# Two transformer blocks in split fp32r precision: three 256-wide matmuls per k-tile in place of a 512-wide and a 256-wide one

## What is computed

```
# block 1                                          # block 2
z = rms_norm(x) @ w_in          # 2048 x 11264      proj = rms_norm(x) @ w_in_2       # 2048 x 9216
y_a = hgrn2_scan(...) * silu(hg)  # 8 heads         y_a = gmlp(u, v)                  # 8 groups
y_b = chunk_band_attention(...)   # 16 heads        y_b = neighbourhood_attn(...)     # 16 heads
merged = gate_a * (y_a @ w_branch_a) + gate_b * (y_b @ w_branch_b)
h = x + merged @ w_out                              (the same in block 2)
h = h + relu(rms_norm(h) @ w_up)**2 @ w_down        x = x + (silu(gate) * val) @ w_down_2
                                                    # gate, val: 3-tap convolution of rms_norm(x) @ w_up_2
```

## Time and profile before

| | us |
|---|---|
| median of 3 runs | 3141.75 |
| lowest and highest | 3140.42, 3149.58 |
| the profiled execution's span | 3139.2 |
| its first matmul starts after | 9.2 |

### The profile page before, as it was taken

The page is one execution under the profiler, slowest core; times in us unless marked ns, Lnnn a source line. Parts: engine busy times, 40 slices in busy tenths (PEclk is TensorE's granted clock), DMA queues, the critical chain, the costliest instruction groups (busy, mean ns, idle before and its releaser), DMA issues.

```text
span 3139.2 us, 53753 instructions
## 1 busy us (share of the span) xinstructions
PE 2927.3 (93%) x16379; PEld 2496.7 (80%) x16379; DVE 2169.0 (69%) x3324; ACT 1515.2 (48%) x2293; POOL 1680.3 (54%) x1105
## 2 busy tenths in 40 slices
PE   5999999989999999999988999899899999999997
PEld 4777777778788888888876777777787788888886
DVE  5777777777568655556577666656747888878885
ACT  5544555556444444444463444445555444444454
POOL 4444445445655666656673445444374455555554
PEclk9999999999999999999999999999999999999998
DMA  5455555545556666666754555565565566666664
GB/s 160 144 146 145 145 145 146 146 140 165 172 173 177 191 190 186 185 183 192 202 148 135 151 155 162 144 163 154 155 188 156 166 182 183 189 177 190 187 182 123
DMA packets 1016035, 519.81 MB, mean 166 GB/s; under 512 B 28980, under 2 KB 1014700, under 8 KB 1015596
## 3 DMA queue, kind: packets, MB, share of 16 engines
q1 hardware_dynamic: 1014032, 513.90, 57.5%
q10 hardware_dynamic: 1820, 3.65, 0.3%
HBM read 515.35 MB, written 2.13 MB: 165 GB/s over the span
## 4 chain that ended last, share of the span: by engine, by line
PE 54%; DVE 27%; issue 9%; ACT 7%; DVEq 1%; DMA 0%; ACTq 0%; SPq 0%; POOL 0%; POOLq 0%
PE acc L401 24%; PE acc L403 12%; DVE w_lo L1157 6%; PE psX L401 5%; PE psT L401 5%; ACT w_hi L737 4%; PE psX L403 2%; PE psT L403 2%; DVE work L1163 2%; DVE work L1534 2%; DVE hT L1362 1%; DVE hT L1361 1%; DVE work L1521 1%; DVE work L1520 1%; DVE HS L1280 1%
## 5 line engine op out<-in xcount | busy, mean ns | idle before, releaser
L1049 POOL TENSOR_TENSOR w_lo<-w_raw,w_hi 128x512 fp32r<-128x512 f32 (+1 forms) x960 | 1548.2, 1625 | 1385.5 <-ACT w_hi L737 1381.5
L1157 DVE TENSOR_TENSOR w_lo<-w_raw,w_hi 128x512 fp32r<-128x512 f32 (+1 forms) x960 | 906.6, 950 | 688.6 <-ACT w_hi L737 634.6
L737 ACT ACTIVATE w_hi<-w_raw 128x1024 fp32r<-128x1024 f32 (+1 forms) x960 | 995.4, 1050 | 601.1 <-PE acc L403 467.4
L401 PE MATMUL acc<-XU,w_hi 128*128 128x512 f32 x3488 | 1256.7, 402 | 26.6 <-DVE work L1163 18.7
L403 PE MATMUL acc<-XU,w_lo 128*128 128x256 f32 x3488 | 983.6, 282 | 0.0
L401 PEld LDWEIGHTS acc<-XU,w_hi 128*128 128x128 f32 x3488 | 662.0, 190 | 195.7 <-DVE w_lo L1157 18.5
L401 PE MATMUL acc<-XY,w_hi 128*128 128x512 f32 x2112 | 768.6, 405 | 44.6 <-DVE work L1163 18.4
L403 PEld LDWEIGHTS acc<-XU,w_lo 128*128 128x128 f32 x3488 | 665.5, 191 | 1.1
L403 PE MATMUL acc<-XY,w_lo 128*128 128x256 f32 x2112 | 598.9, 284 | 0.0
L401 PEld LDWEIGHTS acc<-XY,w_hi 128*128 128x128 f32 x2112 | 404.0, 191 | 151.1 <-DVE w_lo L1157 23.6
L403 PEld LDWEIGHTS acc<-XY,w_lo 128*128 128x128 f32 x2112 | 407.2, 193 | 0.1
(11 more groups left out here) (250 smaller groups left out, 2993.5 us busy)
## 6 DMA issues: line engine op xcount, KB each, us to landing
w_raw<-in_w_in SPq DMA_DIRECT2D x320, 512.0 KB, 3.9
w_raw<-in_w_up SPq DMA_DIRECT2D x300, 512.0 KB, 4.4
w_raw<-in_w_down SPq DMA_DIRECT2D x208, 512.0 KB, 4.3
w_raw<-in_w_out SPq DMA_DIRECT2D x64, 512.0 KB, 3.9
w_raw<-in_w_branch SPq DMA_DIRECT2D x32, 512.0 KB, 3.8
w_raw<-in_w_branch_a SPq DMA_DIRECT2D x16, 512.0 KB, 3.8
w_raw<-in_w_branch_b SPq DMA_DIRECT2D x16, 512.0 KB, 3.8
bias<-in_rel_bias SPq DMA_DIRECT2D x8, 384.0 KB, 5.1
```

The source lines that it names most:

```text
L401: nc.tensor.matmul(bank[:, :], hi[:, k, col:col + P], X[:, k0 + k, :], start=first and k == 0, stop=False, skip_group_check=True)
L737: act.activation(w_hi[s][:, 0:n], w_raw[s][:, 0:n], ACT.Copy).then_inc(hi_done, 1)
L1049: nc.gpsimd.tensor_tensor(w_lo[s][:, n // 2:n], w_raw[s][:, n // 2:n], w_hi[s][:, n // 2:n].bitcast(F32), ALU.subtract).then_inc(lo_pool, 1)
L1157: V.tensor_tensor(w_lo[s][:, 0:n // 2], w_raw[s][:, 0:n // 2], w_hi[s][:, 0:n // 2].bitcast(F32), ALU.subtract).then_inc(lo_dve, 1)
```

## The change

In `products` the 512-wide matmul of w_hi becomes two of 256 columns, one with x_hi and one with x_lo, and both go to the left half of the bank, where the third, w_lo with x_hi, goes as before. The right half is not used. With the whole sum in 256 columns there is nothing to add at the tile's end: `copy_cross`, the buffer `cross` and `tile_sum` go. `tile_times` reads the bank and multiplies with the scale or the gate in one VectorE step, which frees the bank; `add_to_residual` has one step for two. VectorE waits for `w_used` where it waited for ScalarE's copy. Semaphores that told of single finished tiles (`hq_z`, `avz_ready`, `conv_z` and others) are replaced by `acc_free`, which counts all tiles (`evicted`). What is waited for, where and how far ahead weights are prepared is unchanged.

```diff
--- before.py
+++ after.py
@@ products, TensorE
-                    nc.tensor.matmul(bank[:, :], hi[:, k, col:col + P], X[:, k0 + k, :],
-                                     start=first and k == 0, stop=False, skip_group_check=True)
+                    nc.tensor.matmul(bank[:, 0:T], hi[:, k, col:col + P], X[:, k0 + k, 0:T],
+                                     start=first and k == 0, stop=False)
+                    nc.tensor.matmul(bank[:, 0:T], hi[:, k, col:col + P], X[:, k0 + k, T:2 * T],
+                                     start=False, stop=False)
                     done = nc.tensor.matmul(bank[:, 0:T], lo[:, k, col:col + P], X[:, k0 + k, 0:T],
-                                            start=False, stop=last and k == nk - 1, skip_group_check=True)
+                                            start=False, stop=last and k == nk - 1)
@@ ScalarE
-            def copy_cross(p, i, c, b, bank):
-
-                act.wait_ge(w_used, p.block(i, b) + 1)
-                act.activation(cross[:, c % 2, :], bank[:, T:2 * T], ACT.Copy).then_inc(cross_ready, 1)
...
-            def sigmoid_of(n, wait_name, done_name, i):
-                act.wait_ge(S(wait_name), i + 1)
+            def evicted(p, i, t):
+                act.wait_ge(acc_free, p.tile(i, t) + 1 + TILE_CREDIT)
+
+            def sigmoid_of(n, t, done_name, i):
+                evicted(ph["heads1"], i, t)
                 act.activation(wk(4), wk(n), ACT.Sigmoid).then_inc(S(done_name), 1)
@@ VectorE
-            def tile_sum(p, i, c, b, t, bank, dst):
-
-                dve.wait_ge(cross_ready, p.cross(i, c) + 1)
-                mark(V.tensor_tensor(dst, bank[:, 0:T], cross[:, c % 2, :], ALU.add), acc_free,
-                     p.tile(i, t) + 1 + TILE_CREDIT)
-
-            def scaled_tile(p, i, c, b, t, bank, dst, s, value):
-
-                tile_sum(p, i, c, b, t, bank, dst)
-                mark(V.tensor_tensor(dst, dst, rs[:, :], ALU.mult), s, value)
+            def tile_times(p, i, b, t, bank, dst, by):
+
+                dve.wait_ge(w_used, p.block(i, b) + 1)
+                mark(V.tensor_tensor(dst, bank, by, ALU.mult), acc_free, p.tile(i, t) + 1 + TILE_CREDIT)
+
+            def scaled_tile(p, i, b, t, bank, dst):
+
+                tile_times(p, i, b, t, bank[:, 0:T], dst, rs[:, :])
+
+            def scaled_gate(p, i, n, b, t, bank):
+
+                tile_times(p, i, b, t, bank[:, 0:T].rearrange("p (a t) -> p a t", a=1), G[:, ds(i * 4 + n, 1), :],
+                           rs[:, :].rearrange("p (a t) -> p a t", a=1))
...
                         z = work[:, at + half:at + half + 1, 0:T]
-                        tile_sum(p, i, b, b, b, four_banks[b % 4], wk(at + half))
                         gate = G[:, ds(gate_of(i, b), 1), :]
                         dve.wait_ge(S(f"gates_ready{x}"), i * 16 + b + 1)
-                        link(V.tensor_tensor(z, z, gate, ALU.mult))
+                        tile_times(p, i, b, b, four_banks[b % 4][:, 0:T].rearrange("p (a t) -> p a t", a=1), z, gate)
...
                 dve.wait_ge(w_used, p.block(i, b) + 1)
                 h = hT[:, ds(j, 1), :]
-                link(V.tensor_tensor(h, bank[:, 0:T].rearrange("p (a t) -> p a t", a=1), h, ALU.add))
-                mark(V.tensor_tensor(h, bank[:, T:2 * T].rearrange("p (a t) -> p a t", a=1), h, ALU.add), acc_free,
+                mark(V.tensor_tensor(h, bank[:, 0:T].rearrange("p (a t) -> p a t", a=1), h, ALU.add), acc_free,
                      p.tile(i, t) + 1 + TILE_CREDIT)
```

More of the change, by code:

```diff
@@ L42, with __init__ @@
 class Phase:
-    def __init__(self, name, before, iters, blocks, tiles, crosses, shapes=None):
-        self.name, self.iters, self.blocks, self.tiles, self.crosses = name, iters, blocks, tiles, crosses
+    def __init__(self, name, before, iters, blocks, tiles, shapes=None):
+        self.name, self.iters, self.blocks, self.tiles = name, iters, blocks, tiles
         fives = next(n for n in range(blocks) if (blocks - 5 * n) % 4 == 0)
@@ L135, in phases @@
             ("ffn1last", 1, *ffn_counts("ffn1last"), None),
-            ("gmv", 1, 16, 8, 8, None), ("heads2", HEADS, 16, 8, 8, None),
-            ("branch2", 2, 16, 16, 16, None), ("out2", 2, 16, 8, 0, None),
+            ("gmv", 1, 16, 8, None), ("heads2", HEADS, 16, 8, None),
+            ("branch2", 2, 16, 16, None), ("out2", 2, 16, 8, None),
             ("ffn2first", 1, *ffn_counts("ffn2first"), tail),
@@ L141, in phases @@
     out, before = {}, None
-    for name, iters, blocks, tiles, crosses, shapes in plan:
-        before = out[name] = Phase(name, before, iters, blocks, tiles, crosses, shapes)
+    for name, iters, blocks, tiles, shapes in plan:
+        before = out[name] = Phase(name, before, iters, blocks, tiles, shapes)
     return out
@@ L458, in job @@
                         pe.wait_ge(S(read), i + 1)
-                    pe.wait_ge(S(wait_name), i + 1)
+                    if tile is not None:
+                        evicted(ph[wait_name], i, tile)
+                    else:
+                        pe.wait_ge(S(wait_name), i + 1)
                     for a in range(NT):
@@ L903, in ffn1 @@
             def ffn1(name, i):
-                p, tile, c = ph[name], 0, 0
+                p, tile = ph[name], 0
                 for b, s in enumerate(FFN[name]):
```

125 lines of the change are left out of this document (44 added, 81 removed).

## The result

The changed kernel takes **3097.37 us** in the median (3095.65 to 3100.24), the kernel before, on the same chip, 3145.45 us (3140.42 to 3149.58). The ratio is 0.9843, with a 95% interval from 0.9824 to 0.9862: 1.6% faster, where 2.4% was forecast. The time is inside the stated range of 3025 to 3145 us, 2 us above the narrower span of the forecast (3035 to 3095), and a good third of the gain is missing.

What follows compares the result with a forecast made beforehand. TensorE's matmul pairs bound ffn1 and nearly ffn2; elsewhere TensorE waited for VectorE and ScalarE. Profiled 3139.2 us, less 8 for matmuls and 68 for waits, plus 2.5 to the median, gave 3065 us; 8 in 10 range 3025 to 3145.

Steps and rivals of the forecast that it cites:

- The stream: TensorE's matmuls in all 7,696 k-tiles: three narrow steps of 116.7 ns, 350 ns for 351, -8 us in all.
- the slow end: Rival, TensorE's matmuls: three steps of 120 ns, +69 us against 68 saved, 3141 us, no change; chance 0.10.
- third load not hidden: Rival, TensorE's k-tiles: first two narrow steps cost 124 to 130 ns each, k-tile 365 to 377, 3225 us; chance 0.13.
- low clock: TensorE after long waits: less time at the 1.2 GHz level where waits get shorter, 3 us saved.
- back-to-back gap: Trainium skill's formula for a warm TensorE matmul step: N/2.4 plus 2.5 ns, 327.5 ns per k-tile after 325, +19 us.
- rule on row groups: Trainium skill, TensorE: a weight load overlaps a running matmul only if its row group differs; 0.11 us per k-tile, +850 us.
- The waits: TensorE's waits for VectorE and ScalarE tile work, the heads above all: 76 us less, taken as -68 us.
- the last tenth: Deduction from the 76 us saved in waits: a shortened chain meets the next, so nine tenths were taken, -68 us.
- heads1 25: heads1: shorter chains to the log gates' transposes 11 us, decay products 12, the iteration's tail 2; 25 us saved.
- heads2 8: heads2: 8 x 0.46 us of a 13.4 us wait and 8 x 0.58 of a 9.4 us wait; 8 us saved.
- the branches 12: branch1, branch2: VectorE's two-block round falls from 6.40 to 5.1 us, TensorE sets the pace; 6.2 us each, 12 saved.
- ffn2first 11: ffn2first: VectorE makes low weights in time, so "issue" waits of 9.4 us and 2 of earlier ones go; 11 us saved.

Runs made afterwards that it cites:

- reading-only kernel: The changed kernel with the 512 and 256 wide matmuls of before, the product of high weights and low data left out of the result; 3033.99 us, ratio 0.9646.
- the cut alone: The kernel before with its 512-wide matmul cut into two of 256, halves still summed as before; 3192.19 us, ratio 1.0154.
- the other order of loads: The changed kernel with the low weights' matmul between the two with the high weights; 3098.91 us, ratio 0.9859.

## Why the prediction was right in its sign and short in its size

**The stream: the term that failed.** The prediction took 350 ns a k-tile, -8 us, with bounds of -92 and +69. It is 360 ns and +69 us, the slow end of its bounds. The step was "three narrow steps, 3 x 116.7". That length had been read from narrow steps that stand behind a wide one. In the quick rhythm the pair has 230 - 213.3 = 16.7 ns above the columns at the wide step and 10 at the narrow one; their mean is 13.3, and 13.3 is what each matmul of 256, 320 and 512 columns has when it stands among its like. The surplus goes with the number of matmuls; how a pair shares it out says nothing of a third. So 320 + 3 x 13.3 = 360 could have been worked out from the earlier trace rows. The slow rhythm of before (353.3 ns) is 6.7 ns above this rule. It stays in the reading-only kernel, whose stream is 2701 us as before, and is in none of those with equal widths. What makes it stays open.

**The rival "third load not hidden" and the slow end.** The rival put 124 to 130 ns on each of the first two steps; it was wrong in size, right in its suspicion that the surplus isn't a property of the narrow step, and of the two signs named for it one is there (ffn1 at 560 or above) and one is not (steps of 0.125 us or more). The slow end had the stream right, with 0.10, and gave 3141 us, since it set 68 us of waits against it. Waits and low clock together were 109. (Two of the sums are off by a little: the slow end's terms give 3143 us, and the low end of the range of all terms, 92 and 95 us off, is 2955 and not 2963. Neither changes a reading.)

**The Trainium skill.** In this sum it had the better sign: its formula for the back-to-back gap (TensorE: Matmul & The Clock Gate, Back-to-back issue gap), which that section gives for a matmul by itself, puts 2.5 ns on each, an estimate of +19 us for the third. But what the runs show is 13.3 ns above the columns, five times as much. Its rule on row groups (Part 3, The mechanism) would by the prediction's estimate have cost 0.11 us a k-tile; the trace does not agree: the changed kernel's loads start while a matmul runs, all on 128 rows, and the k-tile grew by 9 ns.

**The waits: right, and too careful.** Predicted -68 us, of these 3 for the low clock and the last tenth held back. Measured -93 and -16. Stage by stage, before the tenth:

- heads1 25: 27 measured. The chains named are the ones that shrank (22.2 to 4.2 us, 13.9 to 3.3); by the reading alone they go to 8.2 and 5.6, that is by 14.0 and 8.3 us, where 11 and 12 were priced. A new one took part of it: TensorE's wait for the low part of the log gates (L1249) is 12.8 us in 8, where 9.3 in 7 stood before.
- heads2 8: 15. Two rows were each priced at one removed step, 3.7 us of 13.4 and 4.6 of 9.4; they fell by 5.9 and by 7.8 us. That is not a longer chain than was thought: in the reading-only run they fall by 4.7 each (to 8.7 and 4.7 us), close to the prices, and with the cut alone by 1.2 and 3.2.
- the branches 12: 21, and the wait of 5.56 us at out1's start is gone, not 1.5 us. A round of two blocks was to fall to 5.1 us of VectorE's work; the timeline of VectorE in branch1 shows it waiting for the next weights:

```profile
754.12 0.69 DVE L1138 TENSOR_TENSOR w_lo<-w_raw,w_hi 128x512 fp32r<-128x512 f32 x1 [0.76 <-ACT w_hi L740]
754.73 0.42 DVE L1144 TENSOR_TENSOR work<-psX,G 128x256 f32<-128x256 f32 x1
755.18 1.06 DVE L1325 TENSOR_TENSOR work<-work 128x256 f32<-128x256 f32 x1
757.00 0.69 DVE L1138 TENSOR_TENSOR w_lo<-w_raw,w_hi 128x512 fp32r<-128x512 f32 x1 [0.75 <-ACT w_hi L740]
757.61 0.42 DVE L1144 TENSOR_TENSOR work<-acc,G 128x256 f32<-128x256 f32 x1
758.21 0.92 DVE L1328 TENSOR_TENSOR XU<-work,XU 128x256 f32 x1 [0.18 <-DVE work L1144]
```

  A block is 757.00 - 754.12 = 2.88 us, which is 8 k-tiles of 360 ns: TensorE sets the pace, as forecast, at its own slower step.
- ffn2first 11: 15, with no "issue" left; ffn1first 5 and ffn1last 5: 4.7 and 4.2; gmv 3: 2.1; ffn2 and ffn2last 8.0. ffn1 went the other way, 2.6 to 6.7, with one wait of 3.5 us for GpSimd's low weights and one of 2.8 for a residual step.

Part of this is not the reading's: the cut alone hides 25 us of waits behind longer matmuls, and the reading alone takes 82 (211 to 129), where 73 stood before the tenth. A term that lengthens the stream and one that shortens waits aren't independent, and the prediction summed them as if they were. Its two errors have opposite signs, 77 us too little for the stream and 41 too much left in waits and clock. That the time came out so near the forecast is in part luck: with the stream as it was and the waits as forecast it would have been 3143 us, no change.

**VectorE.** The new tile step takes 417 ns, the 0.42 of the prediction. VectorE's time fell by 315 us and not by 385, to 1853.7 and not to about 1,780. The missing 70 us have three places. Groups of lines over the whole program, first two of before, then three of the changed kernel:

```profile
L1520 DVE SCALAR_TENSOR_TENSOR work<-work,convc 128x256 f32<-128x256 f32 x86 | 42.3, 491 | 3.3
...
L1395 DVE SCALAR_TENSOR_TENSOR work<-work 128x256 f32<-128x256 f32 x64 | 27.3, 426 | 2.2
```

```profile
L1486 DVE SCALAR_TENSOR_TENSOR work<-work,convc 128x256 f32<-128x256 f32 x86 | 103.5, 1203 | 0.5 <-issue 0.5
...
L1369 DVE SCALAR_TENSOR_TENSOR work<-work 128x256 f32<-128x256 f32 x64 | 62.5, 977 | 2.2
...
L1325 DVE TENSOR_TENSOR work<-work 128x256 f32<-128x256 f32 x32 | 31.5, 985 | 1.1
```

The first step of the convolution took 491 ns before, behind a multiplication of 987 ns; now it is the first SBUF step behind the tile step and takes 1203: 61 us more. In the ffn1 stages the square of the positive part went the same way, from 426 to 977 ns, 35 us, and in the branches the sum of the two gated tiles, 17 us. By their own times the removed steps had 395 us and not 385; against the 113 us the splits of the weights got 24 us shorter and other steps 8. The prediction had priced a removed operation by its own mean, though it knew that the excess above 0.43 was GpSimd's; the excess stays and moves to the next step. It cost the time little where TensorE sets the pace.

**ScalarE**'s copies were worth nothing by their time, as forecast. Nor does VectorE's new wait for the block's matmuls show as a delay: TensorE waited 3.5 us for VectorE's low weights before, and in the changed kernel the list of waits has no such row.

## What to carry to other kernels

Count the matmuls, not only their columns: a cut that leaves the columns as they are still paid for each new matmul here, 13.3 ns against the quick rhythm of before, 6.7 against the slow one and 9 in the mean. Where TensorE has no gaps that is the whole bill, while in the stages full of waits more than half of it was hidden. Make such a change by stage: the form that spares the reading engine where TensorE waits, the wide form where it doesn't (3070 us, against 3097 and 3145). And price a removed step by what its engine does afterwards, not by its own mean: an excess that is a wait for a neighbour passes to the next step in line.

## What the runs showed of the hardware

- Among matmuls of equal width, each with its own weight load, one has a fixed surplus of 13.3 ns over its columns at the full clock, for 256, 320 and 512 columns; at 256 it is so whether the load repeats the one before or not. Every matmul here has its load, so the runs can't say whether the surplus is the load's or the matmul's.
- Below that the step has a floor of about 112 ns, with 224, 192 and (L489) 128 columns alike, near the 0.11 us between two loads from a standing start.
- Steps of alternating width, 512 and 256, have two rhythms at the full clock, 346.7 and 353.3 ns a pair; what sets which is open.
- At the clock's lower level there is no surplus. The kernel with the other order of loads has a stretch with a granted clock of 0.50 (1200.00 to 1200.80 us, behind the last number of busy times):

```profile
1200.00:1200.80 0.80, 0.80 (x6) 0.80 (x5) 0.00 (x0) 0.00 (x0) 0.00 (x0) 0.50 0.63 179
```

Its timeline of matmuls shows 256 columns in 0.21 us, which is 256 at 1.2 GHz:

```profile
1200.25 0.41 PE L396 MATMUL acc<-XY,w_hi 128*128 128x256 f32 x1
1200.46 0.41 PE L398 MATMUL acc<-XY,w_lo 128*128 128x256 f32 x1
1200.67 0.41 PE L400 MATMUL acc<-XY,w_hi 128*128 128x256 f32 x1
```

- A VectorE step with both inputs in SBUF that starts while GpSimd's split of weights runs ends about 0.28 us after that split (L1486: 61 of 86, 1503 ns against 473 for the others), while one that reads the accumulator keeps its 0.42 us. So the excess falls on the first SBUF-only step behind a read of the accumulator, and the next one has none (1.07 us, then 0.41).
